# Routing keys written out over all slots by ACT, and roots two tiles behind the gate products on POOL

## The chip, the cores and the metric

The kernel runs on one core of a Trainium2 chip. The metric is the device time of one execution, in microseconds (us). The engines are named as in the profile: PE is TensorE, DVE is VectorE, ACT is ScalarE, POOL is GpSimd and SP is SyncE, which here only issues DMAs.

## The reference

One layer of a streaming encoder for 1152 tokens (1024 of a prompt and 8 x 16 of running streams), in nine tiles of 128 tokens. After a mixing block come product-key experts and a final norm:

```python
q = (h @ wq).reshape(N, 8, 2, 128)
s = einsum('nhpc,hpkc->nhpk', q, keys)            # 128 keys for each half
sv, si = top_k(s, 16)
comb = sv[:, :, 0, :, None] + sv[:, :, 1, None, :]
cv, ci = top_k(comb.reshape(N, 8, 256), 16)       # the best 16 pairs of each head
i1 = take_along_axis(si[:, :, 0], ci // 16)       # the key of the pair's first half
i2 = take_along_axis(si[:, :, 1], ci % 16)        # and of its second
expert, gate = i1 * 128 + i2, softmax(cv)
ff = sum over heads and slots of gate * gelu(u[expert] . h) * v[expert]
x = x + gate2 * ff
y = x * rsqrt(mean(x * x) + 1e-6) * g_final
```

## The kernel before, in words

The program has four blocks, one after the other: modulation, mixing, `routing` and `experts`. The change is in the last two.

**`routing`** ranks the nine tiles one after the other. Each engine runs a list of periods. In period t DVE *chooses* for tile t (`two_lists`, `best_pairs`, `chosen_ranks`, `softmax`), PE and ACT *prepare* the scores of tile t + 1 (`product`, `turn`, `scores` on PE, `take_q` and `take_qT` on ACT), and the tile t - 1 that is *done* is used. Periods 5 to 7 are one loop in the program, the others are written out.

- If the done tile is one of the first four (`PICKED`), its experts are fetched row by row. POOL issues the indirect DMAs for tile 0's 128 slots (`fetch`), and DVE takes a dot product for each (`use`, L1068), 32 in each of the periods 1 to 4.
- If it is one of the last five, it is *placed*: its gates are laid out as a dense table, in 16 batches of 8 tokens. For each batch DVE compares keys with a ramp (`right_hot`, L1090, and `left_hot`, L1093), POOL multiplies the first by the gates (`right`, L840), ACT copies the second (`left`, L890), PE multiplies both (`place_ps`, L1178) and ACT takes the product of the batch before out of PSUM (`take_gates`, `dense`, L900). `left_hot`, `left`, `right_hot` and `right` have two buffers each.

DVE works a done tile off between its own steps: `rows(b)` with b from 0 to 15 stands at sixteen places of its choosing and issues batch b's hot rows, or two dot products. ACT's order within a placing period is written out by hand: for each b `left_rows(b)`, `take_gates(b - 1)`, and at certain b a take of q or qT and the softmax's exponential.

The part of `chosen_ranks` that changes turns ranks into keys. `hit` (which shares memory with `work`) is a comparison of each chosen rank with a ramp of 16 (L1037). Each half of `hit` is multiplied by the 16 best keys of its list (L1045), whose operand repeats every key 16 times by a step of 0 in the innermost dimension, and the 16 products are folded into one (L1051, L1053). The two lists' keys are interleaved in `best_key`, written by L970. `own.settle()` makes DVE wait for its own marked instructions.

**`experts`** multiplies all experts with the last five tiles (PE, 64 pairs of 128-expert blocks) and adds the picked rows of the first four. At its end each tile n goes through a chain over four engines: POOL multiplies the sum by a gate (L1455), DVE adds the residual (`add_x1`, L1677), ACT sums the squares (L1529), DVE makes the mean (`mean_of`, L1681), POOL takes the root (L1459), DVE normalises (`normed`, L1689), and SP stores. DVE's `finish(n)` issues `add_x1(n - 1)`, `mean_of(n - 2)` and `normed(n - 3)`; the first six of them stand between the last pair's ten additions out of PSUM (`collect`, L1569). The gate product of tile 3 waits for all rows of the picked experts (L1595 on DVE), those of tiles 4 to 8 for two `collect` each, and those of tiles 0 to 2 for sums that were read back earlier.

Of the kernel before, what the change touches and what calls it, by code (L numbers as in the profile page):

```python
# [6 lines left out]
BF16 = mybir.dt.bfloat16  # L7
U32 = mybir.dt.uint32
ALU = mybir.AluOpType
# [3 lines left out]
P = 128  # L13
# [4 lines left out]
TILES = 9  # L18
# [7 lines left out]
HEADS = 8  # L26
# [670 lines left out]
def routing(nc, ctx, wq, keys, u_table, v_table, ident_in, shared, h2_rows, h2T_tiles, gate_blocks, picks):  # L697
# [3 lines left out]

    S = sems(nc, "route", "passed consts wq experts_in iota h2 keys_ps keysT q_ps q qT_ps qT scores "
                               "scores_used shifted exp gate_ready keyed slotsT_ps slotsT left_hot left "
                               "right_hot right place_ps placed out0 out1 dve expert picked row_in used "
                               "u0 u1 u2 u3 u4 u5 u6 u7")
    HP = HEADS * 2
    WIDE, NARROW = 4, 12
# [2 lines left out]
    with ExitStack() as mem:  # L710
# [10 lines left out]
        best = sbuf(nc, mem, "best", [P, HP, TOPK])  # L721
        best_at = sbuf(nc, mem, "best_at", [P, HP, TOPK], U32)
        best_key = sbuf(nc, mem, "best_key", [P, HP, TOPK], BF16)
        pair = sbuf(nc, mem, "pair", [P, HEADS, TOPK])
        pair_at = sbuf(nc, mem, "pair_at", [P, HEADS, TOPK], U32)
        soft = sbuf(nc, mem, "soft", [P, HEADS, TOPK])
# [127 lines left out]
        @block.scalar  # L854
        def _(act):
            act.sem_inc(S.placed, 2)
            act.wait_ge(S.keys_ps, 1)
            nc.scalar.activation(keysT[:, :, :], s_ps[:, :, :], ACT.Copy).then_inc(S.keysT, 1)

            def take_q(t, b):  # L860
                n = t * 4 + b
                act.wait_ge(S.q_ps, n + 1)
                wait(act, S.qT_ps, n)
                nc.scalar.activation(q[:, :, :].rearrange("p a c -> p (a c)"), q_ps[:, :], ACT.Copy).then_inc(S.q, 1)

            def take_qT(t, b):
                act.wait_ge(S.qT_ps, t * 4 + b + 1)
                wait(act, S.scores, t * 4)
                nc.scalar.activation(qT[:, b * 4:b * 4 + 4, :], x_ps[:, :, :], ACT.Copy).then_inc(S.qT, 1)

            def take_slots(t):
                act.wait_ge(S.slotsT_ps, t + 1)
                nc.scalar.activation(keyT[:, :, :], x_ps[:, 0:2, :], ACT.Copy).then_inc(S.slotsT, 1)
                nc.scalar.activation(gateT[:, :], x_ps[:, 2, :], ACT.Copy).then_inc(S.slotsT, 1)

            def take_index(t):

                act.wait_ge(S.slotsT_ps, t + 1)
                nc.scalar.activation(idsT[:, t, :], x_ps[:, 0, :], ACT.Copy).then_inc(S.slotsT, 1)
                if t < MIXED:  # L880
                    nc.scalar.activation(gatesT[:, t, :], x_ps[:, 2, :], ACT.Copy).then_inc(S.slotsT, 1)
                else:
                    nc.scalar.activation(gatesT[:, t, :], slots[:, 2, :, :].rearrange("p h k -> p (h k)"), ACT.Copy)\
                        .then_inc(S.slotsT, 1)

            def left_rows(d, b):

                act.wait_ge(S.left_hot, d * BATCHES + b + 1)
                wait_for_placed(act, d, b)
                nc.scalar.activation(left[b % 2][:, :, :], left_hot[b % 2][:, :, :].rearrange("p i t -> p t i"),  # L890
                                     ACT.Copy).then_inc(S.left, 1)

            def take_gates(d, b):
                half = b * 2 // BATCHES
                if b * 2 % BATCHES == 0:
                    wait(act, stored[half], d * 16)
                for g in range(2):
                    act.wait_ge(S.place_ps, (d * BATCHES + b) * 2 + g + 1)
                    at = b * BATCH % BLOCK + g * 4
                    nc.scalar.activation(dense[half][:, :, at:at + 4].rearrange("p i t -> p t i"),  # L900
                                         place_ps[:, g, :, :], ACT.Copy).then_inc(S.placed, 1)

            def period(choose, done, prepare):
                indexed, placed = split(done)
                if prepare is not None:
                    take_q(prepare, 0)
                if indexed is not None:
                    take_index(indexed)
                if placed is not None:
                    take_slots(placed)  # L910
                if prepare is not None:
                    take_qT(prepare, 0)
                    take_q(prepare, 1)
                for b in range(BATCHES):
                    if placed is not None:
                        left_rows(placed - PICKED, b)
                        if b:
                            take_gates(placed - PICKED, b - 1)
                    if prepare is not None and b in (4, 8):
                        take_q(prepare, b // 4 + 1)  # L920
                    if prepare is not None and b in (1, 5, 9):
                        take_qT(prepare, b // 4 + 1)
                    if choose is not None and b == 12:
                        act.wait_ge(S.shifted, choose + 1)
                        nc.scalar.activation(soft[:, :, :], soft[:, :, :], ACT.Exp).then_inc(S.exp, 1)
                if placed is not None:
                    take_gates(placed - PICKED, BATCHES - 1)
            for b in range(4):
                take_q(0, b)
                take_qT(0, b)  # L930
            periods(act, period)

        @block.vector
        def _(dve):
            own = Order(dve, S.dve)
            PER_TILE = 141
            dve.wait_ge(S.iota, 2)
            dve.wait_ge(S.keysT, 1)

# [6 lines left out]
            def two_lists(t, rows):  # L946

                for n in range(HP):
                    if n % 4 == 0:
                        dve.wait_ge(S.scores, t * 4 + n // 4 + 1)  # L950
                        dve.sem_inc(S.passed, 1)
                    own.mark(nc.vector.max(best[:, n, low], s_ps[:, n, :]))
                own.settle()
                dve.sem_inc(S.passed, 1)
                for n in range(HP):
                    own.mark(nc.vector.max_index(best_at[:, n, low], best[:, n, low], s_ps[:, n, :]))
                    own.mark(nc.vector.match_replace(work3[:, n, :], best[:, n, low], s_ps[:, n, :], NEG))
                rows(0)
                own.settle()
                nc.vector.memset(total[:, :], 0.0).then_inc(S.scores_used, 1)  # L960
                for n in range(HP):
                    own.mark(nc.vector.max(best[:, n, high], work3[:, n, :]))
                rows(1)
                own.settle()
                dve.sem_inc(S.passed, 1)
                for n in range(HP):
                    own.mark(nc.vector.max_index(best_at[:, n, high], best[:, n, high], work3[:, n, :]))
                rows(2)
                own.settle()
                own.mark(nc.vector.tensor_copy(best_key[:, :, :], best_at[:, :, :]))  # L970
                rows(3)
                own.settle()

            def best_pairs(t, rows):

# [31 lines left out]
            def chosen_ranks(t, rows):  # L1007
# [5 lines left out]
                for n, (op, by) in enumerate(((ALU.logical_shift_right, 4), (ALU.bitwise_and, 15),  # L1013
# [25 lines left out]
                    .to_broadcast([P, HP, TOPK, TOPK]),  # L1039
                    iota_rank[:, :, :].rearrange("p (o a) k -> p o a k", o=1)  # L1040
                    .to_broadcast([P, HP, TOPK, TOPK]), ALU.is_equal))
                rows(15)
                own.settle()
                for s in range(2):
                    own.mark(nc.vector.tensor_tensor(  # L1045
                        hit[:, s * HEADS:(s + 1) * HEADS], hit[:, s * HEADS:(s + 1) * HEADS],
                        key4[:, :, s, :].rearrange("p h (a o) -> p h a o", o=1)
                        .to_broadcast([P, HEADS, TOPK, TOPK]), ALU.mult))
                own.settle()
                for n in (8, 4, 2):  # L1050
                    own.then(nc.vector.tensor_tensor(hit[:, :, 0:n, :], hit[:, :, 0:n, :], hit[:, :, n:2 * n, :],  # L1051
# [174 lines left out]
def experts(nc, ctx, u_table, v_table, g_final, ident_in, shared, mod_rows, x1_rows, h2_rows, sums_rows, gate_blocks,  # L1226
# [22 lines left out]
    with ExitStack() as mem:  # L1249
# [145 lines left out]
        def _(pool):  # L1395
# [47 lines left out]
            pool.wait_ge(S.gate2_0, 16)  # L1443
            pool.wait_ge(S.gate2_1, 16 * STREAMS)
            pool.wait_ge(S.zero, 2)
            for n in range(TILES + 1):
                if n < TILES:
                    t = FINAL[n]
                    if t >= PICKED:
                        pool.wait_ge(S.y_free, RING + (PAIRS - 1) * OUTPUTS + (t - PICKED) * 2 + 2)  # L1450
                    elif t >= MIXED:
                        pool.wait_ge(S.used, ROWS)
                    else:
                        pool.wait_ge(sums_in[t], 16)
                    pool.tensor_tensor(total(t), total(t), gate2[int(t == TILES - 1)], ALU.mult)\  # L1455
                        .then_inc(S.weighted, 1)
                if n:
                    pool.wait_ge(S.mean, n)
                    pool.tensor_tensor(rstd[:, n - 1:n], mean[:, n - 1:n], power[:, :], ALU.pow).then_inc(S.rstd, 1)  # L1459

        @block.scalar
        def _(act):
# [408 lines left out]
```

## Time and profile before

| | |
|---|---|
| median of 3 runs | 3500.63 us (3499.84 to 3502.5) |
| the profiled execution's own time | 3505.46 us |
| its span, first to last instruction | 3503.8 us |
| busy, share of the span | PE 87%, DVE 70%, POOL 42%, ACT 26% |
| mean granted clock of PE | 0.946 |

A view's row gives an instruction's start in us from the start of the span, its duration, engine, line, operation and tiles. "[0.20 <-ACT left L890]" is idle time before it and what ended it, and "<-issue" is idle time for which the profile shows no cause. A row with "x2" merges two neighbours.

### The profile page before, as it was taken

The page shows a single profiled execution, that of the slowest core. Times are in us where ns is not written, and L with a number is a line of the kernel's source. Part 1 is how long each engine was busy: PE and PEld are TensorE (multiplying, and loading weights), DVE is VectorE, ACT ScalarE, POOL GpSimd, SP SyncE. Part 2 cuts the span into 40 slices and gives each one's busy share as a digit, 9 for nine tenths or more (in the row PEclk, how much of TensorE's full clock was granted, in tenths as well). Part 3 has the DMA queues.
Part 4 walks back from the last instruction along what each step waited for, and adds up shares of the span by engine and source line. Part 5 has one row for each costly group of instructions (what it writes and reads, how often), then busy time and mean ns, then how long its engine had stood idle before and what let it go on. Part 6 is the DMA issues. An engine that isn't in the chain of part 4 may idle for free.

```text
span 3503.8 us, 45737 instructions
## 1 busy us (share of the span) xinstructions
PE 3054.5 (87%) x16658; PEld 2340.8 (67%) x16658; DVE 2447.1 (70%) x4977; ACT 904.3 (26%) x1254; POOL 1477.5 (42%) x1188
## 2 busy tenths in 40 slices
PE   8899969454577556999999999999999999999995
PEld 1466634222355455888888788888788888999994
DVE  1233317999988994777777677776777777788886
ACT  0111111000466783222212122222222212222221
POOL 0000001555444565555454555544555554333334
PEclk9899989777799888999999999999999999999997
DMA  9611142666222337999998999999999998777775
GB/s 360 181 61 60 66 175 72 211 236 224 74 89 102 144 144 296 335 338 330 328 337 306 347 327 335 332 325 321 341 337 327 331 337 304 232 236 236 234 231 192
DMA packets 305762, 858.00 MB, mean 245 GB/s; under 512 B 25360, under 2 KB 108816, under 8 KB 303840
## 3 DMA queue, kind: packets, MB, share of 16 engines
q0 software_dynamic: 151344, 551.09, 44.3%
q1 hardware_dynamic: 154189, 305.27, 25.2%
q8 instruction: 52, 0.85, 0.1%
q14 instruction: 69, 0.57, 0.0%
q10 hardware_dynamic: 108, 0.22, 0.0%
HBM read 793.34 MB, written 63.15 MB: 244 GB/s over the span
## 4 chain that ended last, share of the span: by engine, by line
PE 57%; POOL 2%; DMA 1%; DVE 1%; issue 1%; ACT 0%; DVEq 0%; SPq 0%
PE y_ps L1749 25%; PE a_ps L1730 24%; PE picked_ps L1767 5%; PE uT_ps L1717 3%; DMA shared<-in_peer_u,ids 1%; DMA gates<-gate_blocks 1%; POOL shared L1407 0%; POOL quad L1417 0%; POOL shared L1455 0%; POOL rstd_d L1459 0%; DVE quad L1595 0%; DMA quad<-in_peer_v,idsT 0%; POOL quad L1455 0%; DVE shared L1569 0%; DVE shared L1582 0%
## 5 line engine op out<-in xcount | busy, mean ns | idle before, releaser
L1407 POOL DMA_INDIRECT shared<-in_peer_u,ids x384 | 444.1, 1157 | 641.5 <-DVE acts L1582 594.9
L1730 PE MATMUL a_ps<-h_hi,uT_lo 128*128 128x320 f32 x2048 | 643.8, 314 | 1.7 <-DVE h_lo L1665 1.7
L1730 PE MATMUL a_ps<-h_hi,uT_hi 128*128 128x320 f32 x2048 | 633.8, 309 | 0.0
L1730 PE MATMUL a_ps<-h_lo,uT_hi 128*128 128x320 f32 x2048 | 633.7, 309 | 0.0
L1569 DVE TENSOR_TENSOR shared<-shared,y_ps 128x512 f32<-128x512 f32 x640 | 436.0, 686 | 271.8 <-PE y_ps L1749 271.8
L1749 PE MATMUL y_ps<-v_hi,m_lo 128*128 128x512 f32 x1280 | 510.1, 399 | 14.4 <-DVE shared L1569 9.9
L1749 PE MATMUL y_ps<-v_lo,m_hi 128*128 128x512 f32 x1280 | 505.8, 395 | 0.0
L1749 PE MATMUL y_ps<-v_hi,m_hi 128*128 128x512 f32 x1280 | 503.0, 393 | 0.0
L1582 DVE CUSTOM_DVE_ANT_0 shared<-shared 128x1024 f32<-128x1024 f32 x384 | 464.4, 1219 | 22.6 <-DMA shared<-in_peer_u,ids 22.4
L1417 POOL DMA_INDIRECT quad<-in_peer_v,idsT x384 | 409.5, 1066 | 117.6 <-issue 117.6
L1730 PEld LDWEIGHTS a_ps<-h_hi,uT_lo 128*128 128x128 f32 x2048 | 386.1, 189 | 7.1 <-issue 2.1
L1730 PEld LDWEIGHTS a_ps<-h_lo,uT_hi 128*128 128x128 f32 x2048 | 386.1, 189 | 4.9
L1730 PEld LDWEIGHTS a_ps<-h_hi,uT_hi 128*128 128x128 f32 x2048 | 385.4, 188 | 0.0
L1480 ACT ACTIVATE m_all<-a_ps 128x320 f32<-128x320 f32 x256 | 112.0, 438 | 920.3 <-PE a_ps L1730 920.3
L840 POOL TENSOR_TENSOR right<-right_hot,gateT 128x1024 f32<-128x1024 bf16 x80 | 225.4, 2821 | 206.0 <-DVE right_hot L1090 159.6
L1749 PEld LDWEIGHTS y_ps<-v_hi,m_lo 128*128 128x128 f32 x1280 | 242.1, 189 | 99.3 <-issue 39.4
L1178 PE MATMUL place_ps<-left,right 128*128 128x128 f32 x1280 | 177.3, 296 | 135.4 <-ACT dense L900 69.9
L1471 ACT ACTIVATE uT_hi<-uT_ps 128x512 fp32r<-128x512 f32 x254 | 138.1, 596 | 599.7 <-PE uT_ps L1717 599.7
L1407 POOL DMA_INDIRECT shared<-in_peer_v,ids x128 | 149.3, 1167 | 327.3 <-DVE quad L1595 289.4
L1749 PEld LDWEIGHTS y_ps<-v_hi,m_hi 128*128 128x128 f32 x1280 | 242.4, 189 | 53.9
L1178 PEld LDWEIGHTS place_ps<-left,right 128*128 128x128 f32 x1280 | 164.1, 207 | 160.4 <-issue 91.2
L1749 PEld LDWEIGHTS y_ps<-v_lo,m_hi 128*128 128x128 f32 x1280 | 242.2, 189 | 40.6
(179 smaller groups left out, 4427.5 us busy)
## 6 DMA issues: line engine op xcount, KB each, us to landing
shared<-in_peer_u SPq DMA_DIRECT2D x128, 512.0 KB, 6.4
v_all<-in_peer_v SPq DMA_DIRECT2D x128, 512.0 KB, 6.2
gate_blocks<-dense SPq DMA_DIRECT2D x10, 4096.0 KB, 11.7
gates<-gate_blocks SPq DMA_DIRECT2D x64, 640.0 KB, 17.4
w_ada<-in_w_ada SPq DMA_DIRECT2D x12, 2048.0 KB, 12.1
x_in<-in_x_prompt SPq DMA_DIRECT2D x16, 512.0 KB, 4.3
shared<-in_w_in SPq DMA_DIRECT2D x8, 768.0 KB, 13.7
shared<-in_peer_wq SPq DMA_DIRECT2D x3, 2048.0 KB, 14.2
```

What stands on the lines that cost most here:

```text
L840: nc.gpsimd.tensor_tensor(right[b % 2][:, :, :], right_hot[b % 2][:, :, :].rearrange("p i t -> p t i"), gateT[:, b * BATCH:(b + 1) * BATCH ...
L1178: last = nc.tensor.matmul(place_ps[:, g, j, :], right[b % 2][:, g * 4 + j, :], left[b % 2][:, g * 4 + j, :], start=True, stop=True)
L1407: pool.indirect_dma_start(out=rows[n % 4], out_offset=None, in_=u_table if n < DOTS else v_table, in_offset=bass.IndirectOffsetOnAxis(ap=i ...
L1417: pool.indirect_dma_start(out=quads[half][q], out_offset=None, in_=v_table, in_offset=bass.IndirectOffsetOnAxis(ap=idsT[:, t, token:token ...
L1471: nc.scalar.activation(uT_hi[s][:, n * 4:n * 4 + 4, :], uT_ps[:, n * 4:n * 4 + 4, :], ACT.Copy)\
L1480: nc.scalar.activation(m_all[j][parity][:, n * GROUP:(n + 1) * GROUP], a_ps[n][:, 0:GROUP], ACT.Gelu).then_inc(S.gelu, 1)
L1569: nc.vector.tensor_tensor(part, part, y_ps[n % RING][:, :], ALU.add).then_inc(S.y_free, 1)
L1582: nc.vector.tensor_tensor_reduce(out=rows[n % 4], in0=rows[n % 4], in1=token_row, scale=1.0, scalar=0.0, op0=ALU.mult, op1=ALU.add, accum_ ...
L1717: last = nc.tensor.transpose(uT_ps[:, k, :], u[s][:, k * P:(k + 1) * P], ident[:, :])
L1730: last = nc.tensor.matmul(a_ps[n][:, 0:GROUP], lhs[s][:, k, :], rhs[:, k, tok], start=k == 0 and m == 0, stop=k == KD - 1 and m == 2)
L1749: last = nc.tensor.matmul(y_ps[n % RING][:, :], lhs[j][parity][:, tok], rhs[j][parity][:, col], start=j == 0 and m == 0, stop=j == 1 and m ...
L1767: last = nc.tensor.matmul(picked_ps[n][q * 32:(q + 1) * 32, :], spread[:, half, q, :], quads[half][q][:, n * HALF:(n + 1) * HALF], start=o ...
```

## The change

Routing: a new tile `key_wide` holds the 16 keys of each head, each repeated 16 times. ACT writes it twice per tile (`widen_keys`), once for each list: the first time at batch 6 of its period, when DVE has written `best_key`, the second time at batch 14, when DVE's first product has read the first keys. DVE's two products then read `key_wide`. The first of them stands ahead of `rows(15)` now and the second behind it. `best_key` and the first product leave DVE's own count (`PER_TILE`) and have semaphores of their own.

The end of `experts`: POOL takes the root of tile n - 2 behind the gate product of tile n, and not that of tile n - 1.

```diff
+        key_wide = sbuf(nc, mem, "key_wide", [P, HEADS, TOPK, TOPK], BF16)
...
+            def widen_keys(t, s):
+
+                act.wait_ge(S.best_key, t + 1)
+                if s:
+                    act.wait_ge(S.first_keyed, t + 1)
+                else:
+                    wait(act, S.keyed, t)
+                nc.scalar.activation(key_wide[:, :, :, :],
+                                     key4[:, :, s, :].rearrange("p h (a o) -> p h a o", o=1)
+                                     .to_broadcast([P, HEADS, TOPK, TOPK]), ACT.Copy).then_inc(S.key_wide, 1)
...
                         take_qT(prepare, b // 4 + 1)
+                    if choose is not None and b == 6:
+                        widen_keys(choose, 0)
                     if choose is not None and b == 12:
                         act.wait_ge(S.shifted, choose + 1)
                         nc.scalar.activation(soft[:, :, :], soft[:, :, :], ACT.Exp).then_inc(S.exp, 1)
+                    if choose is not None and b == 14:
+                        widen_keys(choose, 1)
...
-            PER_TILE = 141
+            PER_TILE = 139
...
                 own.settle()
-                own.mark(nc.vector.tensor_copy(best_key[:, :, :], best_at[:, :, :]))
+                wait(dve, S.key_wide, t * 2)
+                nc.vector.tensor_copy(best_key[:, :, :], best_at[:, :, :]).then_inc(S.best_key, 1)
                 rows(3)
-                own.settle()
...
+                own.settle()
+                dve.wait_ge(S.key_wide, t * 2 + 1)
+                nc.vector.tensor_tensor(hit[:, 0:HEADS], hit[:, 0:HEADS], key_wide[:, :, :, :], ALU.mult)\
+                    .then_inc(S.first_keyed, 1)
                 rows(15)
-                own.settle()
-                for s in range(2):
-                    own.mark(nc.vector.tensor_tensor(
-                        hit[:, s * HEADS:(s + 1) * HEADS], hit[:, s * HEADS:(s + 1) * HEADS],
-                        key4[:, :, s, :].rearrange("p h (a o) -> p h a o", o=1)
-                        .to_broadcast([P, HEADS, TOPK, TOPK]), ALU.mult))
+                dve.wait_ge(S.key_wide, t * 2 + 2)
+                own.mark(nc.vector.tensor_tensor(hit[:, HEADS:HP], hit[:, HEADS:HP], key_wide[:, :, :, :], ALU.mult))
+                dve.wait_ge(S.first_keyed, t + 1)
                 own.settle()
...
-            for n in range(TILES + 1):
+            for n in range(TILES + 2):
...
-                if n:
-                    pool.wait_ge(S.mean, n)
-                    pool.tensor_tensor(rstd[:, n - 1:n], mean[:, n - 1:n], power[:, :], ALU.pow).then_inc(S.rstd, 1)
+                if n >= 2:
+                    pool.wait_ge(S.mean, n - 1)
+                    pool.tensor_tensor(rstd[:, n - 2:n - 1], mean[:, n - 2:n - 1], power[:, :], ALU.pow)\
+                        .then_inc(S.rstd, 1)
```

## Rows read from the trace of the kernel before

**Rows 1.** Busy time by stage: PE, PEld, DVE, ACT, POOL, clock, DMA share, GB/s.
```profile
593.30:908.80 315.50, 143.18 (x459) 71.54 (x457) 313.86 (x1132) 22.26 (x45) 173.22 (x128) 0.75 0.66 220
908.80:1264.50 355.70, 236.52 (x1356) 179.23 (x1356) 322.14 (x996) 258.08 (x227) 184.57 (x64) 0.89 0.25 102
...
1345.00:3450.00 2105.00, 2083.96 (x12479) 1754.59 (x12479) 1563.00 (x2399) 476.80 (x784) 1009.27 (x896) 0.99 0.89 310
3450.00:3503.80 53.80, 19.71 (x60) 14.43 (x60) 28.96 (x38) 10.35 (x18) 28.01 (x16) 0.63 0.37 136
```

**Rows 2.** Timeline of DVE in period t = 1: start, duration, line.
```profile
619.36 0.29 DVE L970 CAST best_key<-best_at 128x256 bf16<-128x256 uint32 x1
...
662.57 1.21 DVE L1068 CUSTOM_DVE_ANT_0 dense<-dense 128x1024 f32<-128x1024 f32 x1
...
663.71 4.48 DVE L1045 TENSOR_TENSOR work<-work,best_key 128x2048 bf16<-128x2048 bf16 x2
```

**Rows 3.** Groups by line and shape, 500 to 1340 us: busy us, mean ns.
```profile
L890 ACT ACTIVATE left<-left_hot 128x1024 f32<-128x1024 bf16 x80 | 171.1, 2139 | 52.5 <-DVE left_hot L1093 52.5
...
L1051 DVE TENSOR_TENSOR work<-work 128x2048 bf16<-128x2048 bf16 x9 | 11.0, 1225 | 0.3
...
L858 ACT ACTIVATE keysT<-s_ps 128x2048 f32<-128x2048 f32 x1 | 1.9, 1877 | 18.0 <-PE s_ps L1128 18.0
```

**Rows 4.** Busy time of a stretch of period t = 6, columns as in rows 1.
```profile
1034.00:1081.00 47.00, 37.77 (x259) 30.63 (x258) 46.59 (x99) 47.00 (x41) 32.09 (x12) 1.00 0.25 101
```

**Rows 5.** Timeline of DVE at the end of period t = 6, and in t = 8.
```profile
1067.99 2.60 DVE L1093 TENSOR_TENSOR left_hot<-keyT,iota_keys 128x1024 bf16<-128x1024 bf16 x1 [0.20 <-ACT left L890]
1070.52 2.28 DVE L1037 TENSOR_TENSOR work<-rank,iota_rank 128x4096 bf16<-128x4096 bf16 x1
1072.72 2.91 DVE L1090 TENSOR_TENSOR right_hot<-keyT,iota_keys 128x1024 bf16<-128x1024 bf16 x1
1075.55 0.68 DVE L1093 TENSOR_TENSOR left_hot<-keyT,iota_keys 128x1024 bf16<-128x1024 bf16 x1
1076.15 6.71 DVE L1045 TENSOR_TENSOR work<-work,best_key 128x2048 bf16<-128x2048 bf16 x2
...
1093.98 0.30 DVE L952 MAX8 best<-s_ps 128x8 f32<-128x128 f32 x1 [7.45 <-issue]
...
1248.51 4.49 DVE L1037 TENSOR_TENSOR work<-rank,iota_rank 128x4096 bf16<-128x4096 bf16 x1
```

**Rows 6.** Timeline of POOL at the same place in t = 6.
```profile
1071.17 3.91 POOL L840 TENSOR_TENSOR right<-right_hot,gateT 128x1024 f32<-128x1024 bf16 x1 [1.12 <-PE place_ps L1178]
```

**Rows 7.** Timeline of ACT in periods t = 1 and t = 6.
```profile
619.15 0.60 ACT L864 ACTIVATE q<-q_ps 128x512 f32<-128x512 f32 x1 [4.55 <-PE q_ps L1140]
...
1075.36 2.09 ACT L900 ACTIVATE dense<-place_ps 128x512 f32<-128x512 f32 x2
```

**Rows 8.** Timeline of DVE at the end.
```profile
3434.50 6.00 DVE L1595 SCALAR_TENSOR_TENSOR quad<-shared,mT,quad 128x1024 f32<-128x1024 f32 x1
...
3463.84 1.23 DVE L1677 TENSOR_TENSOR quad<-quad,shared 128x1024 f32<-128x1024 f32 x1 [2.45 <-POOL quad L1455]
...
3491.27 1.27 DVE L1689 SCALAR_TENSOR_TENSOR shared<-shared,rstd_d,quad 128x1024 f32<-128x1024 f32 x1
```

**Rows 9.** Timeline of POOL at the end.
```profile
3434.62 4.78 POOL L1455 TENSOR_TENSOR quad<-quad 128x1024 f32<-128x1024 f32 x2
3460.87 0.58 POOL L1459 TENSOR_TENSOR rstd_d<-mean_d,power_d 128x1 f32<-128x1 f32 x1 [21.47 <-DVE mean_d L1681]
...
3466.70 2.36 POOL L1455 TENSOR_TENSOR quad<-quad 128x1024 f32<-128x1024 f32 x1
...
3491.43 1.52 POOL L1459 TENSOR_TENSOR rstd_d<-mean_d,power_d 128x1 f32<-128x1 f32 x1 [1.40 <-DVE mean_d L1681]
3492.93 2.33 POOL L1455 TENSOR_TENSOR shared<-shared,quad 128x1024 f32<-128x1024 f32 x1
```

**Rows 10.** Timeline of PE at the end.
```profile
3450.34 0.80 PE L1749 MATMUL y_ps<-v_hi,m_lo 128*128 128x512 f32 x1 [4.37 <-DVE m_lo L1555]
```

More of the change, by code:

```diff
@@ L703, in routing @@
                                "scores_used shifted exp gate_ready keyed slotsT_ps slotsT left_hot left "
-                               "right_hot right place_ps placed out0 out1 dve expert picked row_in used "
+                               "right_hot right place_ps placed out0 out1 best_key key_wide first_keyed dve expert picked row_in used "
                                "u0 u1 u2 u3 u4 u5 u6 u7")
```

## The prediction

> **What bounds the kernel now.** I read the page first (engine shares and the 40 slices), then the busy time by stage, then the timelines of the two stages that the change touches. By stage [rows 1], 2105 us of the span belong to the expert products, where TensorE is busy for 2084 us: nothing there changes, and any time won or lost before it moves it bodily. Two stages of routing are DVE's. From 593.3 to 908.8 us DVE is busy for 313.9 of 315.5 us: these are the periods t = 1 to 4, in which DVE ranks tile t and takes dot products of fetched rows between the steps. What shortens DVE there shortens the kernel. From 908.8 to 1264.5 us (t = 5 to 8, in which an earlier tile is also placed) DVE is busy for 322 us of 356, ACT for 258. The last 53.8 us are the finish of nine tiles.
>
> In the placing periods the share hides the limit. In the stretch from 1034 to 1081 us of period t = 6, ACT is busy for 47.00 of 47.00 us [rows 4], and DVE waits for ACT's `left` (0.20 us) before its hot row of batch 14 [rows 5]. Some of DVE's busy time is also blocking: while POOL multiplies into `right`, a DVE instruction with two operands in SBUF takes 2.60, 2.91 or, for the first key product, some 4.5 us, where it takes 0.68 or 2.28 us alone [rows 2, 5, 6].
>
> **DVE's two key products.** They run over 2048 bf16 elements each and take 4.48 us together [rows 2]; the innermost step of their key operand is 0. The first fold after them, also 2048 bf16 elements out of a tensor operation, but with both operands at step 1, takes 1.225 us [rows 3]. With keys written out over all slots the products have that form. I price them at 1.23 us each, 2.53 us with two waits of about 0.04 us: 1.95 us off per tile. The bounds are 0 (they stay at 2.28 us) and 2.1 us.
>
> **ACT's copies.** New on ACT are two copies per tile of 2048 elements, read with step 0. No row has such a read. The nearest contiguous one is `keysT`, 2048 elements from PSUM: 1.88 us. The dearest is `left`, 1024 bf16 elements read with a step of 8: 2.14 us, hence 4.2 us for 2048 [rows 3]. I take 1.88 us, since reading the same element sixteen times stays in one place, unlike `left`, and keep 4.2 us as the other end. [...]
>
> **Periods t = 1 to 4.** The first copy waits for `best_key`. Queued behind it on ACT are the last take of q and of qT, for which TensorE waits, and then the scores of the next tile. In t = 1 `best_key` starts at 619.36 us and that take of q at 619.15 us [rows 2, 7], so it slips by some 2.4 us, while DVE wants the scores only after the key products, past 668.2 us [rows 2]: hidden by 45 us of DVE's own work, and free. The second copy waits for the first product (`first_keyed`) and is needed by the second. Between the two products DVE now does the two dot products of `rows(15)`, 1.14 us from start to start [rows 2], 2.3 us together. The copy with its semaphores needs about 2.0 us: hidden, with 0.3 us to spare. At 4.2 us it would not be, and DVE would wait 1.9 us, all that the faster products give. Gain: 4 x 1.95 = **7.8 us**. In t = 0 there are no rows between, so product, copy, product take 1.23 + 2.0 + 1.23 = 4.5 us as before: 0.
>
> **Periods t = 5 to 7.** ACT has no idle time from 1034 us on, and the first copy sits at batch 6, inside that stretch. It pushes every later `left` back by 1.85 us (1.88 less the overlap of neighbours). DVE's `left_hot` waits for the `left` two batches before it, so the comparison, which starts at 1070.52 us, starts about 1.85 us later and ends at 1074.65. POOL's product that waited behind the comparison [rows 6] then runs as before, to 1077.0, the first product to 1078.2, and the two hot rows to 1079.4. ACT, also 1.85 us late, ends the takes of batch 13 (1075.36 + 2.09 before, [rows 7]) at 1079.3 and copies until 1081.1. POOL's last product (2.4 us from 1079.4) ends at 1081.8. The second product so ends at 1083.0; before it ended at 1082.86 [rows 5]. The faster products are given back to ACT's queue: **0 us**, bounds 2 us either way per period. The late `left` and takes of batch 15 delay TensorE's next product by 4 us, but DVE idles for 7.45 us at the loop's return [rows 5] and then ranks the next lists before its first hot row, so that is free. In t = 8 the comparison itself was blocked (4.49 us, [rows 5]), so POOL's product is already out of the way when the first product comes, and ACT's lateness reaches DVE only in part. I take the middle between 0, as in t = 5 to 7, and 2.1 us: **1 us**.
>
> **The end.** Before, POOL did the products of tiles 0 and 1 at 3434.62 us and then waited 21.47 us for the first mean [rows 9]. Now the product of tile 2 follows at once. But during those two products DVE's row update took 6.00 us, which is 4.78 + 1.27 [rows 8, 9]: it stood still. A third product makes it stand 2.4 us longer. DVE has no idle time from there to `m_lo`, for which TensorE waits 4.37 us [rows 10], so the last second products start 2.4 us late. [...]
>
> In return DVE's addition for tile 2 no longer waits 2.45 us for its product [rows 8]: from 3461.39 + 2.4 = 3463.8 us it does the addition and the normalisation (1.15 and 1.2 us from start to start) and frees POOL's product of tile 3 at 3466.25 us; before, that started at 3466.70 [rows 9]. From there on each tile needs, one after another, the gate product 2.33, the addition 1.2, and the normalisation 1.27, none beside another. Only the root leaves the chain: its 1.52 us [rows 9] are mostly waiting for the normalisation that started 0.16 us before it at 3491.27 [rows 8], which ends at 3492.54, while the next product starts at 3492.93. So 0.39 us per tile for the products of tiles 4 to 8: 5 x 0.39 + 0.45 = **2.4 us**. Bounds: a loss of 2.4 us if nothing comes back, and a gain of 12 us if POOL's products could run beside DVE at a period of 2.33 + 1.52 = 3.85 in place of 5.25 us (7 x 1.4 = 9.8, and the 2.4 not lost).
>
> **Sum.** 7.8 + 0 + 1.0 + 2.4 = 11.2 us. The profiled execution took 3505.46 us (span 3503.8), so it would take 3494.3. The median of the runs is 3500.63, 4.8 us less than the profiled one; I carry the difference over: **3489.4 us**, 0.32% less.
>
> **Rivals.**
> - (a) *ACT's queue eats more in the placing periods.* Both copies then count, 1.9 us lost in each of t = 5 to 7, and nothing won in t = 8: 7.8 - 5.7 + 2.4 = 4.5 us less, 3496. For it: ACT's 47.00 of 47.00. Against: only the first copy lies ahead of the comparison, and the second runs while POOL blocks DVE anyway.
> - (b) *ACT reads step 0 at the price of `left`.* Copies of 4.2 us: t = 0 loses 2.3, t = 1 to 4 come out even, t = 5 to 7 lose 4.1 each, t = 8 2.4, the end wins 2.4, so 14.6 us more: 3515, slower. It decides from a copy of about 2.3 us on, where `rows(15)` no longer covers it; on a line between the two sums the gain is gone at 2.9 us. For it: ACT's other strided copy is that dear. Against: the operand stays in place.
> - (c) *POOL is not held by DVE at the end*: 12 us won there in place of 2.4, 3480. For it: 1.40 us of idle time before each root. Against: the 6.00 us.
> - (d) *The end only loses*: 7.8 + 1.0 - 2.4 = 6.4 us less, 3494.2. For it: POOL may now stand behind several DVE instructions in a row.
>
> **How the numbers follow.** Runs of this kernel spread over 2.7 us, and about 0.2% (7 us) can be told from no change; faster means below 3493.6. Chances: forecast 0.50, (a) 0.17, (b) 0.11, (c) 0.09, (d) 0.13. Faster: 0.50 + 0.09 and a little under half of (d), 0.64. Same: (a) and most of the rest of (d), 0.24. Slower: (b) and a remnant, 0.12. The range reaches from (c) to beyond (a), 3479 to 3500, and leaves out (b) and the far ends. The forecast's own range is 3484 to 3495.
>
> **What would show it.** Right: key products of 1.23 us, copies of 1.9 us, periods t = 1 to 4 of 77 us and not 79, t = 5 to 7 unchanged within 1 us; at the end one DVE row update of about 8.4 us, gate products 4.8 to 4.9 us apart, and a longer wait of TensorE for `m_lo`. Wrong: copies near 4 us with DVE waiting for ACT before the second product; longer periods t = 5 to 7; gate products under 4 us apart.

## The result and the profile after

The changed kernel took 3472.41 us (median of 4 runs, 3469.26 to 3474.19) beside 3500.24 us for the kernel before on the same chip: a ratio of 0.9917, 95% interval 0.9904 to 0.9929. A second time, again beside the kernel before, it took 3470.74 us, 0.9920 (0.9907 to 0.9934). It is faster, by 28 us where 11 were forecast. 3472 lies 7 us below the range's lower end of 3479; nearest among the forecasts is rival (c), 3480, whose mechanism did not occur (below).

Busy time by stage, after; the columns are those of [rows 1], the stages periods 1 to 4, periods 5 to 8, and the finish:

```profile
591.60:899.80 308.20, 145.20 (x459) 73.22 (x457) 305.77 (x1132) 37.02 (x53) 166.60 (x128) 0.76 0.66 225
899.80:1236.70 336.90, 242.48 (x1353) 182.39 (x1354) 301.74 (x996) 269.88 (x234) 176.27 (x64) 0.91 0.25 103
...
3420.40:3469.50 49.10, 18.88 (x60) 13.82 (x60) 39.97 (x39) 10.35 (x18) 27.80 (x15) 0.67 0.42 150
```

Periods 1 to 4 went from 315.5 to 308.2 us, 7.3 us where 7.8 was forecast. Periods 5 to 8 went from 355.7 to 336.9: 18.8 us, where 1 was forecast. That is where the miss lies.

Groups by line and shape, 500 to 1340 us, after (busy us, mean ns of one, idle before). The two products and ACT's copies answer to [rows 2, 3]:

```profile
L894 ACT ACTIVATE key_wide<-best_key 128x2048 bf16<-128x2048 bf16 x18 | 35.1, 1950 | 85.1 <-DVE work L1060 67.4 <-DVE best_key L987 17.7
...
L1060 DVE TENSOR_TENSOR work<-work,key_wide 128x2048 bf16<-128x2048 bf16 x9 | 19.2, 2129 | 0.6
L1064 DVE TENSOR_TENSOR work<-work,key_wide 128x2048 bf16<-128x2048 bf16 x9 | 11.4, 1269 | 10.0 <-ACT key_wide L894 10.0
```

The means mix periods. One by one, the copies take 1.90 us up to period 4 and 1.91 to 2.16 in the placing periods; the products take 1.23 us up to period 4, and in the placing periods, beside POOL, 3.24 to 3.30 (the first) and 1.23 to 1.38 (the second). Period 1, DVE and then ACT; between the two products stand the two dot products (not shown), and the second product waits for nothing:

```profile
659.74 1.23 DVE L1060 TENSOR_TENSOR work<-work,key_wide 128x2048 bf16<-128x2048 bf16 x1
...
663.18 1.22 DVE L1064 TENSOR_TENSOR work<-work,key_wide 128x2048 bf16<-128x2048 bf16 x1
...
661.06 1.91 ACT L894 ACTIVATE key_wide<-best_key 128x2048 bf16<-128x2048 bf16 x1 [16.80 <-DVE work L1060]
```

The end of period 6, DVE, which answers to [rows 5]:

```profile
1055.50 2.28 DVE L1053 TENSOR_TENSOR work<-rank,iota_rank 128x4096 bf16<-128x4096 bf16 x1
1057.91 3.24 DVE L1060 TENSOR_TENSOR work<-work,key_wide 128x2048 bf16<-128x2048 bf16 x1
1061.07 0.68 DVE L1107 TENSOR_TENSOR right_hot<-keyT,iota_keys 128x1024 bf16<-128x1024 bf16 x1
1061.68 0.68 DVE L1110 TENSOR_TENSOR left_hot<-keyT,iota_keys 128x1024 bf16<-128x1024 bf16 x1
1064.31 1.37 DVE L1064 TENSOR_TENSOR work<-work,key_wide 128x2048 bf16<-128x2048 bf16 x1 [1.96 <-ACT key_wide L894]
...
1069.66 2.47 DVE L968 MAX8 best<-s_ps 128x8 f32<-128x128 f32 x12 [0.32 <-issue]
```

The second product waits 1.96 us for ACT's second copy, and it ends 82.1 us after the period's first MAX8; before it was 82.6, with 2.2 us of idle time at issue in them. The last row is the surprise: at the loop's return DVE stands still for 0.32 us, not for the 7.45 us of [rows 5]. DVE's waits from 900 to 1340 us (total, times, longest), first after, then before:

```profile
DVE left_hot L1110 <- ACT left L902: 18.4, 25, 1.4
...
DVE work L1064 <- ACT key_wide L894: 8.0, 4, 2.1
...
DVE best L968 <- issue: 0.7, 2, 0.4
```

```profile
DVE best L952 <- issue: 19.4, 4, 7.5
```

The loop of periods 5 to 7 returns twice. Before, DVE stood still at each return for 7.5 us and, three instructions into the ranking, for 2.2 us more; after, it does not. That is 18.7 us, the whole gain of the stage. DVE's waits for ACT's `left` did grow (5.5 us before, 13 times, against 18.4, 25 times), and there are 8.0 us of waits for the copies. What DVE saves in these periods it waits. A run of the kernel before that lacks the idle time at issue (its loop moved by 16 instructions, below) shows it; its periods 5 to 8, in the columns of [rows 1]:

```profile
907.70:1244.45 336.75, 237.32 (x1356) 179.60 (x1356) 324.39 (x996) 258.00 (x227) 183.50 (x64) 0.92 0.26 108
```

After the change DVE is busy there for 22.7 us less (301.7), 8.8 us of it in the key products, and the periods still take 336.9 us.

The end, after, in one timeline of DVE, POOL and PE (answers to [rows 8 to 10]):

```profile
3403.12 8.34 DVE L1613 SCALAR_TENSOR_TENSOR quad<-shared,mT,quad 128x1024 f32<-128x1024 f32 x1
...
3421.30 0.80 PE L1767 MATMUL y_ps<-v_hi,m_lo 128*128 128x512 f32 x1 [5.34 <-DVE m_lo L1573]
```

```profile
3403.23 7.13 POOL L1472 TENSOR_TENSOR quad<-quad 128x1024 f32<-128x1024 f32 x3
...
3432.60 3.32 POOL L1472 TENSOR_TENSOR quad<-quad 128x1024 f32<-128x1024 f32 x1
3435.87 1.53 POOL L1476 TENSOR_TENSOR rstd_d<-mean_d,power_d 128x1 f32<-128x1 f32 x1
3437.38 2.36 POOL L1472 TENSOR_TENSOR shared<-shared,quad 128x1024 f32<-128x1024 f32 x1
3440.96 1.52 POOL L1476 TENSOR_TENSOR rstd_d<-mean_d,power_d 128x1 f32<-128x1 f32 x1 [1.23 <-DVE mean_d L1699]
3442.45 2.38 POOL L1472 TENSOR_TENSOR shared<-shared,quad 128x1024 f32<-128x1024 f32 x1
```

Three early products, one row update of 8.34 us, and PE waits 5.34 us for `m_lo` where it waited 4.37. From tile 3 on the gate products start 4.8, 5.1, 5.1, 5.1 and 4.4 us apart, where before it was 5.2 to 5.3.

All of the difference between the two profiled executions (span 3503.8 and 3469.5 us, -34.3): up to period 1, -1.7; periods 1 to 4, -7.3; from period 5 to the first expert matmul, 441.7 to 423.2, -18.5; the expert products, 2092.8 to 2088.9, -3.9; from the last `a_ps` (the output of the expert products' first matmuls) to the end of `m_lo` (what DVE writes for the last second ones), 7.1 to 9.4, +2.3; from there to the end, 53.6 to 48.3, -5.3. The expert products took 2087.8 to 2092.8 us over all 14 profiled executions of this study, with no relation to the version, and period 1 began at 591.5 to 594.0 us: the -3.9 and the -1.7 are not the change's.

### The profile page after: what moved, and what is told of

The parts are those of the page before. It is cut to its first block, busy times and chain, and to the rows that moved or that the text cites. A ratio compares the mean times of both kernels' runs of the same rounds, so it can differ in the third digit from the quotient of the medians.

```text
span 3469.5 us, 45795 instructions
## 1 busy us (share of the span) xinstructions
PE 3057.1 (88%) x16658; PEld 2341.4 (67%) x16658; DVE 2429.8 (70%) x4977; ACT 935.1 (27%) x1272; POOL 1462.9 (42%) x1188
## 4 chain that ended last, share of the span: by engine, by line
PE 58%; DVE 2%; DMA 1%; POOL 1%; issue 1%; ACT 0%; SPq 0%; DVEq 0%
PE y_ps L1767 25%; PE a_ps L1748 25%; PE picked_ps L1785 5%; PE uT_ps L1735 3%; DMA shared<-in_peer_u,ids 1%; DMA gates<-gate_blocks 1%; DVE quad L1613 0%; POOL shared L1424 0%; POOL quad L1434 0%; DVE shared L1707 0%; DVE shared L1587 0%; DVE shared L1695 0%; DMA quad<-in_peer_v,idsT 0%; DVE quad L1695 0%; DVE quad L1707 0%
## 5 line engine op out<-in xcount | busy, mean ns | idle before, releaser
L841 POOL TENSOR_TENSOR right<-right_hot,gateT 128x1024 f32<-128x1024 bf16 x80 | 217.5, 2720 | 194.8 <-DVE right_hot L1107 121.9
L1568 DVE TENSOR_TENSOR m_all<-m_all,gates 128x320 f32<-128x320 f32 x256 | 126.4, 494 | 199.6 <-ACT m_all L1498 189.6
## 6 DMA issues: line engine op xcount, KB each, us to landing
gate_blocks<-dense SPq DMA_DIRECT2D x10, 4096.0 KB, 11.2
```

Of the source, the lines that this page charges most:

```text
L841: nc.gpsimd.tensor_tensor(right[b % 2][:, :, :], right_hot[b % 2][:, :, :].rearrange("p i t -> p t i"), gateT[:, b * BATCH:(b + 1) * BATCH ...
L1568: nc.vector.tensor_tensor(part, part, gates[c % 2][:, n * per:(n + 1) * per, j, :], ALU.mult)\
```

## The experiments

The idle time at the return is called issue by the profile: it waits for nothing that the profile shows. Two things could have removed it, the place of the loop in DVE's program or what the change did to the instructions in it.
```profile
q14 instruction: 10, 0.08, 0.1%
```

Five packets per turn of the loop, then. They start when DVE is 0, 5, 14, 122 and 254 recorded instructions behind the return; the last two are 132 apart (128 to 136 in the runs below). The loop has 307 recorded instructions, after the change 309. That the ten are DVE's code, the next run shows: it moves nothing but DVE's program, and none is left.

**The kernel before, with the loop moved by 16 and by 100 instructions.** The instructions put ahead (fillers) are `dve.sem_inc` on a count that nothing waits for in these kernels, where DVE is idle anyway:

```diff
             own = Order(dve, S.dve)
             PER_TILE = 141
+            for _ in range(16):          # 100 in the second
+                dve.sem_inc(S.passed, 1)
             dve.wait_ge(S.iota, 2)
```

> The kernel before with 16 one-word semaphore instructions put ahead of routing's part of DVE's program, where DVE waits for its first data anyway; no wait, no operand and no order in the loop is touched. Theory 'place': the 7.5 and 2.2 us in which DVE stands still at each of the two returns of the routing loop are a fetch of its program, and whether one is needed hangs on where the loop lies in that program; 16 instructions move the loop's head to nearly where the changed kernel has it (14 further on). Then the 19.4 us that the chain of waits puts at issue go to under 1 us, the stages t = 5 and t = 6 take 82 to 84 us in place of 91.5 and 93.7, and the time is 3500 - 19 = about 3481 us. Rival 'work': the change took the idle time away by what it did to the instructions in the loop (two wide operands, a moved product, one settling less). Then it stays here and the time is 3500 us.

> The same edit with 100 such instructions. Theory 'place': a move is no gain by itself; on the guess that the program comes in pieces of equal size (the queue that brings it moves packets of 8192 B) and that the loop must lie in few of them, this head lies about as badly as before's. Then some 19 us of standing still remain, the second stall some 30 instructions later in the loop than before's, and the time is 3500 us within 3 us. Rival 'any move helps' (the fillers themselves, or a fetch started earlier): 3481 us. Rival 'work': 3500 us too, with the second stall at the same three MAX8 as before.

Measured: 3484.5 us with 16, ratio 0.9955 (0.9938 to 0.9971); 3499.83 us with 100, 0.9991 (0.9982 to 1.0001). DVE's waits at issue from 900 to 1340 us, with 16 and with 100:

```profile
DVE best L954 <- issue: 0.7, 2, 0.4
```

```profile
DVE best L954 <- issue: 14.9, 2, 7.5
```

Sixteen instructions that do nothing take the idle time away, and a hundred do not. "Work" and "any move helps" are out. With 100 the second stop is gone rather than 30 instructions later: its packet came at 1002.4 us, when DVE was 15 recorded instructions behind the return.

**The changed kernel, moved by 90, 114 and 60.** The same two lines, in the changed kernel.

> The changed kernel with 90 such instructions ahead of routing's part of DVE's program, which puts the loop's head where theory 'place' has it lie badly again. Theory 'place': DVE stands still at the two returns again, some 19 us in all, and the time is 3472 + 19 = about 3491 us, near what the prediction said of the change. Rival 'work': the loop's own instructions took the idle time away, so the time stays at 3472 us.

 Rival 'place and loop': the changed loop's own instructions keep part of the idle time away wherever it lies (as the 5.7 us with 90 fillers would have it): under 8 us stand at issue, and the time is 3475 to 3480 us.

> The changed kernel with 60 fillers ahead of routing's part of DVE's program. In the kernels that stand still at the loop's return, packets of code come some 130 recorded instructions apart in the loop (122 and then 254 in the kernel before), and the loop has 307 to 309. Theory 'pieces': with a packet of 128 instructions the changed loop's head lies 9 instructions into one, with 60 fillers 69, and 69 + 309 = 378 still ends within three pieces (384), where 99 + 309 (90 fillers) needs a fourth. So moving the loop this far is free: no packet of code between the first return and the loop's end, under 1 us at issue, 3472 us. Rival 'lucky place' (only heads near the start of a piece escape): packets and idle time at the returns as with 90 fillers, some 6 us, 3478 us.

Measured: 3478.7 us with 90 (0.9934, 0.9918 to 0.9951), 3482.96 with 114 (0.9948, 0.9932 to 0.9965), 3473.38 with 60 (0.9922, 0.9906 to 0.9939). At issue, in this order:

```profile
DVE best L970 <- issue: 5.7, 2, 2.9
```

```profile
DVE best L970 <- issue: 8.9, 4, 2.9
```

```profile
DVE best L970 <- issue: 0.7, 2, 0.4
```

With 90 and 114 there are five packets per turn again, with 60 none from the first return to the loop's end. So the place decides whether the code is fetched anew. But the sizes of the first two were missed by both theories: not 19 us. The run with 114, whose head lies where before's did if a packet holds 128 instructions, shows how. First its return, DVE and SP, then that of the kernel before:

```profile
984.17 0.29 DVE L1096 TENSOR_TENSOR slots<-soft,total 128x128 f32<-128x128 f32 x1
987.32 0.70 DVE L970 MAX8 best<-s_ps 128x8 f32<-128x128 f32 x3 [2.85 <-issue]
989.80 2.70 DVE L970 MAX8 best<-s_ps 128x8 f32<-128x128 f32 x13 [1.78 <-issue]
...
986.91 0.34 SPq L799 DMA_DIRECT2D gate_blocks<-dense  x1
```

```profile
992.44 0.29 DVE L1077 TENSOR_TENSOR slots<-soft,total 128x128 f32<-128x128 f32 x1
1000.27 0.69 DVE L952 MAX8 best<-s_ps 128x8 f32<-128x128 f32 x3 [7.55 <-issue]
1003.14 2.70 DVE L952 MAX8 best<-s_ps 128x8 f32<-128x128 f32 x13 [2.18 <-issue]
...
989.67 0.34 SPq L798 DMA_DIRECT2D gate_blocks<-dense  x1
```

The second stop is back at the very same instruction, behind three MAX8, and the turn's fourth packet comes 121 and 122 recorded instructions behind the two returns, where in the kernel before it was 122 both times. So a move by 128 instructions (114 fillers and the 14 of the change) is one by a whole packet. The first is shorter, and the difference is the store: before, SP issues a 4096 KB store of `dense` 2.9 us ahead of DVE's branch (992.52 us), and it moves from 990.5 to 1001.3; DVE's first packet comes only at 998.2. In the changed kernel ACT, whose takes release the store and whose queue now holds the copies, releases it 2.65 us behind the branch (984.26), and the packet comes at 985.3.

**The kernel before, with that store held back at the two returns.**

```diff
                     sp.wait_ge(S.placed, d * 32 + 2 + 16 * (half + 1))
+                    if half and d < 2:
+                        sp.wait_ge(S.passed, (d + 6) * 12 + 2)
                     sp.dma_start(gate_blocks[bass.ds(d * 2 + half, 1), :, :, :].rearrange("a p i j -> p (a i j)"),
```

> The kernel before; SP holds the second 4096 KB store of a placed tile back, at the two returns of the loop alone, until DVE is past the first four MAX8 of the next stage. DVE's program is untouched. In the kernel before this store moves from 990.5 to 1001.3 us, DVE branches at 992.52 and its first packet of code comes at 998.2; in the changed kernel with 114 fillers DVE branches at 984.26, the packet comes at 985.3, and the store starts at 987.7: the same place in the program, 2.85 us of idle time and not 7.55. Theory 'fetch behind the store': with the store out of the way the first idle time falls to 2.9 us at each return and the second stays near 2 us: 9 to 10 us at issue in place of 19.4, and 3500 - 9.5 = about 3491 us. Rival 'the loop's own instructions' make the difference between 7.55 and 2.85: 19.4 us stay, and 3500 us.

Measured: 3488.33 us, 0.9965 (0.9952 to 0.9978), and 8.8 us at issue. The first return, DVE and SP:

```profile
991.33 0.29 DVE L1079 TENSOR_TENSOR slots<-soft,total 128x128 f32<-128x128 f32 x1
994.79 0.69 DVE L954 MAX8 best<-s_ps 128x8 f32<-128x128 f32 x3 [3.17 <-issue]
996.90 2.70 DVE L954 MAX8 best<-s_ps 128x8 f32<-128x128 f32 x13 [1.42 <-issue]
...
997.13 0.34 SPq L800 DMA_DIRECT2D gate_blocks<-dense  x1
```

With DVE's program untouched, the first stop falls from 7.55 to 3.17 us. The 19.4 us are therefore 10.6 us of waiting behind the store and 8.8 us of fetching.

The start of the expert products (first `a_ps`, us) puts the runs in one line, free of what comes later: with before's loop 1350.4 (19.4 us at issue), 1347.5 (14.9), 1338.5 (8.8), 1329.9 (0.7); with the changed loop 1330.7 (8.9), 1329.1 (5.7), and 1320.2 to 1324.9 (0.7, seven executions).

**Each part alone.** The changed kernel with POOL's old order at the end, and the kernel before with POOL's new order. Their edits are the last hunk of the change, taken back and made alone.

> The changed kernel with POOL's order at the end put back (root one tile behind the gate product): routing's part alone, with the loop where the change put it. By the traces of before and after, the end's part is worth 2.9 us (5.3 us gained behind m_lo, 2.3 us lost ahead of it), so this takes 3472 + 2.9 = about 3475 us. Rival 'the end does nothing': 3472 us. Within it, stages t = 1 to 4 take 77.0 to 77.4 us as in the changed kernel, and the placing stages 83.5 to 86 us.

> The kernel before with POOL's new order at the end alone; DVE's program is untouched, so routing keeps its 19.4 us at issue and its 79.0 us stages. Expected 3500 - 2.9 = about 3497 us, with a row update of about 8.3 us beside POOL's three early products, and some 48 us from the end of m_lo to the end of the span in place of 53.6. Rival 'the end only loses' (the prediction's rival d): 3502 us.

Measured: 3475.16 us (0.9921, 0.9904 to 0.9937) for the keys alone, 3499.38 (0.9993, 0.9983 to 1.0002) for the end alone. The end's part is too small for the times to settle; the traces agree. From the last `a_ps` to the end of `m_lo` it is 7.1 us with the old order (keys alone) and 9.4 with the new (end alone); from there to the end 53.5 and 48.3. Over all executions that hold no product back it is 7.1 and 9.3 to 9.4, then 52.8 to 53.6 (five with the old order) and 47.2 to 48.5 (six with the new). Rival (d) is out: 2.3 us lost, some 5 won.

**Gate products behind `m_lo`.** In the changed kernel POOL holds back all gate products, or the third alone:

```diff
             pool.wait_ge(S.zero, 2)
+            pool.wait_ge(S.m_lo, PAIRS * 2)          # first version
             for n in range(TILES + 2):
+                if n == 2:
+                    pool.wait_ge(S.m_lo, PAIRS * 2)  # second version, without the line above
                 if n < TILES:
```

> The changed kernel, with POOL's gate products at the end held back until DVE has written its last m_lo. Theory 'port': POOL's third gate product and DVE's last row update (8.34 us in the changed kernel, 6.00 before) hold each other up, and the update is on the path to the end. With the products behind m_lo, m_lo ends 2.3 us sooner or more (up to 7 us: all three of POOL's early products at 7.13 us stand beside DVE's work there), and the products find DVE idle for the first tiles, so the end stands 2 to 7 us earlier: 3465 to 3470 us. Rival 'chain': the end goes at the pace of POOL's gate products from m_lo on, and three products that were done early now stand in that chain at 4.8 to 5.1 us each: 3472 + 5 to 10, less the 2.3 us: about 3475 to 3480 us.

> The changed kernel with the third gate product alone held back until DVE has written its last m_lo; two stay early, as before the change. This tells the end's two terms apart. If the third early product costs what the prediction took (2.4 us on DVE's row update, 8.34 against 6.00 us) and nothing is lost by doing it later, because DVE stands idle for 3 us behind m_lo: m_lo ends 2.3 us sooner and the time is 3472 - 2.3 = about 3470 us, and then holding back the first two as well, as the run before did, was worth about 1 us of its 3 to 4. If the third product is needed early: 3472 to 3474 us.

Measured: 3468.85 us (0.9903, 0.9887 to 0.9920) for all, 3468.03 (0.9902, 0.9885 to 0.9918) for the third alone. The third alone, DVE, PE and POOL:

```profile
3402.64 6.00 DVE L1615 SCALAR_TENSOR_TENSOR quad<-shared,mT,quad 128x1024 f32<-128x1024 f32 x1
...
3418.49 0.79 PE L1769 MATMUL y_ps<-v_hi,m_lo 128*128 128x512 f32 x1 [4.37 <-DVE m_lo L1575]
...
3418.51 2.37 POOL L1474 TENSOR_TENSOR quad<-quad 128x1024 f32<-128x1024 f32 x1 [10.96 <-DVE m_lo L1575]
```

The row update is back at 6.00 us and PE's wait at 4.37, as before the change, and the product that moved costs nothing that shows where it now stands: 47.8 us from `m_lo` to the end, 48.2 in a second execution (48.0 with all held back, 48.3 in the changed kernel). With the other two held back as well, `m_lo` ends 0.5 us sooner (6.5 us behind the last `a_ps`); the time does not show it.

**The changed kernel and the third product held back, side by side.**

> The changed kernel unaltered, timed in the same call as the next run: 3472 us, 0.9917 of before. If the place of the loop is what took the 19 us, its two returns show under 1 us at issue again in this execution.

> The version with the third gate product alone behind the last m_lo, timed beside the changed kernel: 2 to 4 us under it, 3468 to 3470 us, if the 2.3 us that the third early product costs DVE are the path's; the same time as the changed kernel if the earlier difference was that of two calls.

Measured: 3470.74 us (0.9920, 0.9907 to 0.9934) for the changed kernel, with 0.7 us at issue again, and 3467.65 (0.9901, 0.9886 to 0.9916) with the third product held back. All three medians of the versions with products held back lie 2 to 5 us under the changed kernel's two, but the intervals overlap: the 2.3 us are shown by the traces (9.3 and 7.1 us to `m_lo`) and not by the times.

## Why the prediction was wrong

**The step that failed** is in periods t = 5 to 7, "DVE idles for 7.45 us at the loop's return [rows 5] and then ranks the next lists before its first hot row, so that is free". The idle time was used as a cover that stays, with no cause looked for, and the period was closed with 0 us. It was a code fetch whose presence hung on the loop's place in DVE's program, and whose length hung on a store that ACT releases. The change altered both, by accident: the loop's head moved by 14 instructions, and ACT's copies put the store behind the return. The first alone is enough: the kernel before, moved by 16, had 0.7 of its 19.4 us left. The second alone takes some 10 of them (8.9 us at issue with 114 fillers in place of 19.4). No rival had this, so the range did not reach it.

**The rest of the sum held in size, though not everywhere by the way that was told.** From the kernel before with its loop moved (3484.5 us) to the changed kernel (3472.41 and 3470.74) it is 12 to 14 us, against a forecast of 11.2; that run's times spread over 12 us, so the terms are better read from the traces:

- Key products and copies, t = 1 to 4: 7.3 of the 7.8 us, with products of 1.23 us as priced and copies of 1.90 us where 1.88 was taken from `keysT`. Rival (b) is out. The 1.90 us are for 2048 elements read with step 0, beside 2.14 for half as many elements of `left`, read with a step of 8. What makes `left` dear was not shown.
- Periods 5 to 8 apart from the idle time: forecast -1. From the start of period 5 to the first expert matmul the kernel before without idle time took 422.2 us, the executions of the changed loop without it 419.5 to 423.5. So 0 within 3 us. The way was partly another. In t = 5 to 7 the prediction had POOL's product hold the second key product and ACT's second copy done in time; instead the second product waited for that copy, 1.94 to 1.97 us each time. That is what rival (a) said, but its 5.7 us did not come: these three periods took 250.9 to 255.3 us in the seven executions, and 252.8 in the kernel before without idle time. In t = 8 the prediction had POOL's product out of the way of the first key product; that product took 3.30 us beside POOL all the same, and the second waited 2.10 us for the copy. The forecast 1 us came (82.1 to 83.3 us for the period, 83.7 to 84.2 before), but not by the way told, so that agreement is in part luck.
- The end: a row update of 8.34 us where 8.4 was forecast (7.13 of POOL's three products and 1.27 of its own are 8.40; that DVE stands still during POOL's products rests on these times and on the 6.00 us with two products alone, and what holds it was not shown), 2.3 us lost before `m_lo` (2.4 forecast), and 5.3 us won behind it (4.8 forecast: the net 2.4 and the 2.4 lost): 3.0 in place of 2.4. The gate products came 4.4 to 5.1 us apart and 4.9 on the mean, as forecast. The start of tile 3's product, put at 3466.25 us, is 3466.15 by the prediction's own steps; the 0.1 us changes nothing. Rival (c), products under 4 us apart, is out.

So 7.3 + 0 + 3.0 = 10.3 us by the traces for the forecast's own terms, and 18.7 us that it did not have: 29.0, beside 28 in the medians.

## What to carry to other kernels

An idle time that the profile puts at issue, at a loop's return or a few instructions behind it, need be neither fixed nor free (here it was 7.5 and 2.2 us with the loop in one place, and 0.3 to 0.4 us with it in another): look whether the instruction queue moves packets there, and try a few instructions that do nothing ahead of the loop before anything else is changed. An edit to a loop, or to anything ahead of it in the same engine's program, moves the loop; a measured gain or loss of such an edit is worth a second run with the loop moved back. Do not count an idle time as cover without its cause, since the edit may take it away.

## What the runs showed of the hardware

- POOL's root of 128 single elements took 0.57 to 0.58 us beside DVE's addition out of PSUM (after, at 3432.04 us; before, at 3460.87) and 1.52 us beside DVE's normalisation (before, at 3491.43).
- Left open: the same changed program took 86.1 us for period 6 in one execution and 83.8 in another, with nothing in the code between them.
